# Attention's final scaling split in two, the first tile's inversion run beside the sample's heads, and token transposes ahead of score products

## What is computed

```python
h = rmsnorm(x); c = h @ w_in                       # RWKV columns | q, k, v | two gates
# A: RWKV-7 time mixing: a matrix state scanned over the tokens, per head
# B: differential attention, block-causal for the prompt
s = einsum(q, k) * d**-0.5; p = softmax(s)
o = einsum(p[:, 0] - lam * p[:, 1], v)             # per head
o = rmsnorm(o, subln) * (1 - lam_init)             # the "final scaling"
mix = sigmoid(gA) * (y_a @ w_out_a) + sigmoid(gB) * (o @ w_out_b)
x = x + rmsnorm(mix @ w_o)
x = x + rmsnorm((silu(u_g) * u_v) @ w_ffn_out)     # u_g, u_v = rmsnorm(x) @ w_ffn_in
```

## Time and profile before

| | |
|---|---|
| median of 3 runs | 1107.36 us (1107.15 to 1109.85) |
| the profiled execution's own time | 1107.29 us |
| its span, first to last instruction | 1105.5 us |
| TensorE busy | 1011.3 us (91%) |
| VectorE busy | 501.0 us (45%) |
| ScalarE busy | 276.5 us (25%) |
| GpSimd busy | 490.8 us (44%) |
| mean granted TensorE clock | 0.969 of 2.4 GHz |

### The profile page before, as it was taken

One profiled execution on the slowest core, in us unless ns is written; L12 is line 12 of the kernel. 1 busy time (PEld: TensorE's weight loads), 2 busy tenths in 40 slices (PEclk: granted clock), 3 DMA queues, 4 the chain that ended last, 5 costly groups with the idle time before them and its releaser, 6 DMA issues.

```text
span 1105.5 us, 21747 instructions
## 1 busy us (share of the span) xinstructions
PE 1011.3 (91%) x8886; PEld 954.9 (86%) x8886; DVE 501.0 (45%) x859; ACT 276.5 (25%) x768; POOL 490.8 (44%) x327
## 2 busy tenths in 40 slices
PE   4999998899958889989989994999999999999995
PEld 4999998887856777768789994999999999999994
DVE  5566798367565555554348317232332333200003
ACT  4223452255421222423221235110110111010111
POOL 3555564323233113142164550555655556556561
PEclk9999999999979999999999996999999999999997
DMA  8233323422212100002412531233232332332232
GB/s 240 72 90 83 77 77 97 120 59 70 78 60 60 35 2 31 31 13 75 156 49 71 183 95 39 58 94 88 83 95 77 94 89 81 88 89 85 74 86 82
DMA packets 137580, 89.15 MB, mean 81 GB/s; under 512 B 5242, under 2 KB 129504, under 8 KB 137504
## 3 DMA queue, kind: packets, MB, share of 16 engines
q1 hardware_dynamic: 128356, 70.42, 22.5%
q10 hardware_dynamic: 9148, 17.65, 4.5%
HBM read 78.86 MB, written 9.19 MB: 80 GB/s over the span
## 4 chain that ended last, share of the span: by engine, by line
PE 80%; DVE 12%; ACT 2%; issue 2%; POOL 1%; DMA 1%; DVEq 0%; ACTq 0%; POOLq 0%
PE dense L892 64%; PE side L944 4%; PE side L844 1%; PE side L818 1%; PE side L1064 1%; PE side L987 1%; PE side L874 1%; PE side L808 1%; PE side L1013 1%; DVE amax L1509 1%; DVE mb L1803 1%; PE side L839 1%; PE side L798 1%; DVE gain L1452 1%; DVE otok L1536 1%
## 5 line engine op out<-in xcount | busy, mean ns | idle before, releaser
L647 POOL TENSOR_SCALAR w_hi<-w_raw 128x1024 fp32r<-128x1024 f32 x127 | 139.2, 1096 | 484.5 <-PE dense L892 467.0
L650 POOL TENSOR_TENSOR w_lo<-w_raw,w_hi 128x1024 fp32r<-128x1024 f32 x127 | 311.7, 2455 | 10.6
L892 PE MATMUL dense<-h_hi,w_hi 128*128 128x272 f32 x1392 | 306.3, 298 | 10.1 <-DVE h_lo L1445 8.5
L892 PE MATMUL dense<-h_lo,w_hi 128*128 128x272 f32 x1392 | 296.1, 290 | 0.0
L892 PE MATMUL dense<-h_hi,w_lo 128*128 128x272 f32 x1392 | 294.9, 289 | 0.0
L892 PEld LDWEIGHTS dense<-h_hi,w_hi 128*128 128x128 f32 x1392 | 222.9, 191 | 20.1 <-DVE h_lo L1445 9.6
L892 PEld LDWEIGHTS dense<-h_lo,w_hi 128*128 128x128 f32 x1392 | 224.3, 191 | 0.0
L892 PEld LDWEIGHTS dense<-h_hi,w_lo 128*128 128x128 f32 x1392 | 223.4, 191 | 0.0
L892 PE MATMUL dense<-S,w_hi 128*128 128x272 f32 x960 | 162.0, 291 | 1.7 <-DVE S L1806 1.5
L892 PEld LDWEIGHTS dense<-S,w_hi 128*128 128x128 f32 x960 | 136.5, 189 | 2.5 <-DVE S L1806 2.0
L892 PE MATMUL dense<-S,w_lo 128*128 128x272 f32 x480 | 99.5, 289 | 0.0
(11 more groups left out here) (249 smaller groups left out, 1314.9 us busy)
## 6 DMA issues: line engine op xcount, KB each, us to landing
w_raw<-in_w_ffn_in SPq DMA_DIRECT2D x44, 512.0 KB, 3.8
w_raw<-in_w_in SPq DMA_DIRECT2D x43, 512.0 KB, 3.9
w_raw<-in_w_ffn_out SPq DMA_DIRECT2D x16, 448.0 KB, 3.6
gates<-gst ACTq DMA_DIRECT2D x16, 272.0 KB, 2.0
w_raw<-in_w_o SPq DMA_DIRECT2D x8, 512.0 KB, 3.8
w_raw<-in_w_ffn_out SPq DMA_DIRECT2D x8, 512.0 KB, 3.7
mb<-gates ACTq DMA_DIRECT2D x1, 2176.0 KB, 8.8
ga<-gates ACTq DMA_DIRECT2D x1, 2176.0 KB, 9.4
```

The source lines that it names most:

```text
L647: nc.gpsimd.tensor_scalar(w_hi[:, slot, :], w_raw[:, slot, :], 1.0, 0.0, ALU.mult, ALU.add).then_inc(hi_split, 1)
L650: nc.gpsimd.tensor_tensor(w_lo[:, slot, :], w_raw[:, slot, :], w_hi[:, slot, :].bitcast(F32), ALU.subtract).then_inc(w_split, 1)
L892: ins = pe.matmul(acc[:, hf, 0:HALF], w, r[:, hf * HALF:(hf + 1) * HALF], start=first and n == 0, stop=final and n == 2)
```

## The change

Three things in `schedule()`, with the handlers that belong to them. `oscale` becomes two steps: step 0 for the four prompt tiles (it waits for the last prompt head), step 1 for the sample. Tile 0's `sb0`, `xi` and the first 12 of its 15 inversion rows, together with `oA` of tiles 0 to 3, are woven into the rows of the sample's four heads; its last three rows (`wt` 3, `wm` 4, `wd` 4) stay behind the `ofin` steps. In each tile `tok` stands ahead of `sk`, and `xi` of the next tile behind both. The fillers go where the list below says: one behind each `ofin`, three instead of eight in tile 0's inversion, and in tiles 0 to 3 seven instead of five (one more ahead of `sb1`, one more in the weave). No instruction's shape changes.

```diff
     for i, th in enumerate(heads):
-        s += piece() + [("attP", *th)] + piece()
+        rows = [piece() + [("attP", *th)], piece()]
         if i + 1 < len(heads):
-            s += [("attC", *heads[i + 1])]
+            rows[-1] += [("attC", *heads[i + 1])]
         if i + 2 < len(heads):
-            s += [("attS", *heads[i + 2])]
-        s += piece() + [("attO", *th)]
-    s += [("oscale",)]
+            rows[-1] += [("attS", *heads[i + 2])]
+        rows += [piece() + [("attO", *th)]]
+        if th[0] < SAMPLE:
+            s += sum(rows, [])
+        else:
+            sample += rows
...
-    s += invert_head(0)
-    for n, st in enumerate(skew(NT, "oA", "ofin")):
-        s += [st] + filler(n % 2)
-    s += weave([[("init0",)]] + invert_rows(0), [filler(1) for _ in range(8)])
+    first = invert_rows(0)
+    scaled = [[("oA", t)] for t in range(SAMPLE)]
+    s += [("oscale", 0)] + invert_head(0) + weave(sample, first[:-3], scaled)
+    s += [("oscale", 1), ("oA", SAMPLE)]
     for t in range(NT):
-        s += (invert_head(t + 1) if t < SAMPLE else []) + both("sk", t) + both("tok", t) + filler(t == SAMPLE)
-        s += both("sb1", t) + both("gv", t) + both("wu", t) + filler(t == SAMPLE) + both("e", t) + filler(1)
+        s += [("ofin", t)] + filler(1)
+    s += weave([[("init0",)]] + first[-3:], [filler(1) for _ in range(3)])
+    for t in range(NT):
+        head = t < SAMPLE
+        s += (both("sb0", t + 1) if head else []) + both("tok", t) + both("sk", t) + (both("xi", t + 1) if head else [])
+        s += filler(1) + both("sb1", t) + both("gv", t) + both("wu", t) + filler(t == SAMPLE) + both("e", t) + filler(1)
         if t < SAMPLE:
-            s += weave(invert_rows(t + 1), state_rows(t), post_rows(t - 1) if t else [], [filler(1) for _ in range(4)])
+            s += weave(invert_rows(t + 1), state_rows(t), post_rows(t - 1) if t else [], [filler(1) for _ in range(5)])
...
             elif k == "oscale":
-                landed(act, ("attO", SAMPLE, BH - 1), "o")
-                A.mark(f_act(orms[:, 0:SAMPLE * BH], ossq[:, 0:SAMPLE * BH], ACT.Sqrt, scale=1.0 / BV, bias=EPS),
-                       s_["o_rms"], "o_rms")
-                A.mark(f_act(orms[0:DEC, SAMPLE * BH:], ossq[0:DEC, SAMPLE * BH:], ACT.Sqrt, scale=1.0 / BV, bias=EPS),
-                       s_["o_rms"], "o_rms")
+                n, a, b_ = ((P, 0, SAMPLE * BH), (DEC, SAMPLE * BH, NT * BH))[step[1]]
+                landed(act, ("attO", SAMPLE if step[1] else SAMPLE - 1, BH - 1), "o")
+                A.mark(f_act(orms[0:n, a:b_], ossq[0:n, a:b_], ACT.Sqrt, scale=1.0 / BV, bias=EPS), s_["o_rms"], "o_rms")
...
             elif k == "oscale":
-                dve.wait_ge(s_["o_rms"], 2)
-                V(vec.reciprocal(orst[:, 0:SAMPLE * BH], orms[:, 0:SAMPLE * BH]))
-                V(vec.reciprocal(orst[0:DEC, SAMPLE * BH:], orms[0:DEC, SAMPLE * BH:]))
+                n, a, b_ = ((P, 0, SAMPLE * BH), (DEC, SAMPLE * BH, NT * BH))[step[1]]
+                dve.wait_ge(s_["o_rms"], step[1] + 1)
+                V(vec.reciprocal(orst[0:n, a:b_], orms[0:n, a:b_]))
```

More of the change, by code:

```diff
@@ L237, in schedule @@
     s += [("attS", *heads[0]), ("attC", *heads[0]), ("attS", *heads[1])]
+    sample = []
     for i, th in enumerate(heads):
-        s += piece() + [("attP", *th)] + piece()
+        rows = [piece() + [("attP", *th)], piece()]
         if i + 1 < len(heads):
-            s += [("attC", *heads[i + 1])]
+            rows[-1] += [("attC", *heads[i + 1])]
         if i + 2 < len(heads):
-            s += [("attS", *heads[i + 2])]
-        s += piece() + [("attO", *th)]
-    s += [("oscale",)]
+            rows[-1] += [("attS", *heads[i + 2])]
[4 more added lines that the diff above has]
+            sample += rows
     fill = [dense("gA", i, p, 4) for i in range(8) for p in range(4)] + [dense("outB", i, p, 2) for i in range(8) for p in range(2)]
```

## The result

The changed kernel took 1103.09 us in the median of 10 runs (1096.13 to 1105.81), the kernel before 1109.92 us beside it (10 runs): a ratio of 0.994, 95% interval 0.9921 to 0.9959. It is faster, by 6.6 us instead of 19.7, and outside the range of 1078 to 1097 us. The profiled execution took 1105.81 us, span 1104.0 us, mean granted clock 0.956 (before 0.969). It is the slowest of the ten, so its profile shows more of what went wrong than the median does.

The account below looks back on a forecast made before the run. TensorE, busy 91% of the span, was taken as the bound, with its idle and low-clock time removable. Gains of 9.5 + 9.3 + 0.9 = 19.7 us off 1107.3 gave 1088 us, range 1078 to 1097.

Parts of the forecast that it names:

- `tok` ahead of `sk`, tiles 0 to 3: Prompt tiles' heads: four `gt` waits go, 7.3 us, with 0.9 + 1.1 us of low clock: 9.3 us gained.
- The failed step: Sample's stretch: a low clock follows the long wait at the first `wt`, costing 1.5 us.
- the forecast wait: Sample's stretch: TensorE waits 3.4 us at the first `wt` for `xp`.
- The idle time of the sample's stretch: TensorE's new idle time beside the sample's heads: 5.0 us behind VectorE and 3.4 us at `wt`, 8.4 us.
- the first part: Scaling and inversion moved beside the sample's heads: 19.4 us won less 9.9 us of new losses, net 9.5 us.
- the rival of the changed name: Tile heads: ScalarE's copies, or `xi` behind `gt`, are as late as `gt` was; 1097 us, chance 0.10.
- Each piece keeps its price: Fillers: a dense piece costs the same wherever it stands, so moving pieces was counted as no gain or loss.
- the margin that was called thin: Around `outB`: VectorE's 2.4 us wait for `mb` and its drains, 3.9 us, are covered by TensorE's 0.3 + 3.9 us.
- a sign of being wrong: In the changed profile, a wait ending at the load of `mb` (L1792) would show the forecast wrong.
- The end: End of the stage: `yfin` falls inside TensorE's last wait, 4.15 us for `y_lo`, gaining 0.9 us.
- the clock stays low through the mixed stretch: Rival: sample's heads to inversion's end, 15 pieces and 7 us of small work, all at low clock; 1113 us, chance 0.03.
- the sample's stretch gives all back: Rival: new losses in the sample's stretch equal the 19.4 us won there; 1097 us, chance 0.13.

Follow-up runs that it names:

- old head order: Changed kernel with only the tile heads' order undone (`xi`, `sk`, `tok` again) in all tiles: 0.9959 of the kernel before, 1102.41 us.
- 0.9898: Changed kernel with `sk` ahead of `tok` in tile 4 alone, tiles 0 to 3 keeping the new order: ratio 0.9898 to the kernel before, 1097.56 us.
- both measurements of the change: The changed kernel measured, then again without any edit: 0.994 (1103.09 us) and 0.9936 (1100.65 us) of the kernel before.
- twelve pieces: Kernel with `sk` first in tile 4 and four pieces per weave, plus a dense piece in each of the sample's twelve rows: 0.9817, 1089.71 us.
- four-piece weaves: Kernel with `sk` first in tile 4, weaves of tiles 0 to 3 cut from five pieces to four, the rest at the stage's end: 0.9908, 1097.31 us.
- three pieces ahead: Kernel with a piece in each of the sample's twelve rows, three pieces moved from the stage's end ahead of tile 4's score products: 0.9795, 1086.28 us.

## Why the prediction was wrong

The ratios add up to the result in three terms:

| term | forecast | measured | from |
|---|---|---|---|
| scaling and inversion, fillers, end of the stage | 9.5 + 0.9 | 4.6 | old head order, 0.9959 |
| `tok` ahead of `sk`, tiles 0 to 3 | 9.3 | 6.8 | 0.9898 against 0.9959 |
| `tok` ahead of `sk`, tile 4 | 0 | -4.4 | 0.9938 (mean of both measurements of the change) against 0.9898 |
| sum | 19.7 | 7.0 | |

Each is uncertain by 1.6 to 2.5 us, from the intervals.

- **The failed step is the clock.** "A wait of that length is followed by a low clock, as both long waits were: 1.5 us" ties the low clock to long waits, and so gives tile 4 none and the sample's stretch one short spell. The runs showed three things against it. First, no long wait is needed: in tile 4 the clock fell after a start with no wait over 0.97 us, and stayed up longer where a single wait of 1.48 us stood in front of dense work. Second, the forecast wait, that at the first `wt`, isn't the cause in the sample's stretch: filling it left the low clock at 13.7 us, and with twelve pieces it stands unfilled and there is no low clock at all, in three profiles. Third, the second of the two spells there followed a wait of 2.1 us in a place that the forecast didn't name. *The Trainium skill (TensorE: Matmul & The Clock Gate, A second HAM failure mode: psum-queue depth-cycling) describes a kernel, of another shape and type, whose frequent short idles between groups of matmuls make the clock swing; the trace agrees, with 2.24 us busy of 3.30 in front of 17 us at 0.51.*
- **Its price in the sample's stretch** comes from busy times. With twelve pieces and no low clock TensorE was busy 47.2 us; less five pieces of 1.63 that is 39.1 us for the changed kernel's work. It took 42.6, 43.6 and 45.0 us with 6.8, 10.2 and 13.7 us at the low clock: 3.5, 4.5 and 5.9 us, a little under half of the time at the low clock, against the forecast 1.5. The kernel before has the same matmuls in this stretch as the one with twelve pieces and was busy 50.6 us, so its low clock cost 3.3 us, about the 3.5 that the forecast had counted as won. The time at the low clock is about that of before (13.7); but the low clock of before lay partly in idle time, where it cost nothing, and the new one lies in full work. So instead of winning 2.0 us, the clock of this stretch lost 0.2 to 2.6.
- **The size of tile 4's term** was never in the sum. I read the head's order only where it had a `gt` wait, and tile 4 has none: its `tok` is short, ScalarE is late with a store there, and putting `tok` first draws `sk` behind ScalarE's copies: one wait of `tok` of 0.97 us, three of `sk` of 0.52, 0.26 and 0.26. Small waits, 2.0 us in all and no more idle time in the stretch than before, but strung together.
- **The idle time of the sample's stretch** was right in sum, 8.06 us against 8.4, and wrong in place. The first `wt` cost 2.2 us in two waits (1.36 and 0.86), not 3.4. The longest single wait was that of a product `wd` behind VectorE (2.1 us at 312.17), for this reason:

```profile
300.34 1.14 DVE L1542 SCALAR_TENSOR_TENSOR otok<-otok,orst,subln 128x128 f32<-128x128 f32 x4
...
307.48 4.09 DVE L1542 SCALAR_TENSOR_TENSOR otok<-otok,orst,subln 128x128 f32<-128x128 f32 x8
311.60 0.76 DVE L1664 TENSOR_TENSOR gain<-side,cst 128x256 f32<-128x256 f32 x2
```

  Eight scalings stood in VectorE's queue ahead of the drain that TensorE waited for. Four took 1.14 us, eight 4.09 instead of 2.3, since one split of GpSimd (2.38 us from 307.07) fell on them. The forecast had bounded that collision at one split of 2.5 us, and it was one. VectorE's sum was overestimated elsewhere: L1452's successor took 0.43 us a piece, not 0.70. The `ofin` stretch and the last three inversion rows, costed at nothing, lost 0.50 and 0.70 us, which the 8.06 contain.
- **The place of the scaling carries the first part** (1.000 with all scalings behind the sample's root; no run put them behind the rows but ahead of that root). The cover of four pieces in front of the sample's own scaling held: its transpose waits 0.5 us where 3.55 stood, and for a bank (`o_lo` L1451), not for the scaling.
- **The heads of tiles 0 to 3**: the `gt` waits went as forecast. `sk` doesn't wait for ScalarE there. A wait of up to 0.8 us for `rb` at `gv` took a part of the place, 1.4 us in sum, as `xi` now stands ahead of `sb1`'s drain on VectorE; the rival of the changed name had that mechanism with a fifth of its price. The 2.0 us of low clock that the forecast tied to the `gt` waits don't go with them: with the old head order all four stand (7.3 us) and tiles 0 to 3 have no low clock, and the changed kernel has 10.2 us of it there without them. These two are more than the 2.5 us missing, within the intervals.
- **Each piece keeps its price** held by the time for five against four pieces in the weaves, and failed for the place that mattered: five pieces cost 8.2 us at the end and 0.7 us in the sample's stretch.
- **The load of `mb`** used up the margin that was called thin. In the changed kernel VectorE waits 1.98 us for it (forecast 2.4) at 514.32, a wait that the forecast had named as a sign of being wrong, and TensorE 0.83 us behind VectorE's next drain, where nothing had been counted. With a shorter weave it collided with another transfer, in a place that I hadn't named, the store of tile 3's state (6 us).
- **The end** gained 0.5 us (wait for `y_lo` 3.63 instead of 4.15), not 0.9.

Of the rivals, *the clock stays low through the mixed stretch* came nearest to the mechanism, with a chance of 0.03. It didn't hold as priced, 15 pieces all low; about a quarter of the stretch was low, and another spell stood in tile 4. That the sample's stretch gives all back didn't come.

What stays open: what lowers the clock of tile 4 in the kernels with four-piece weaves. With `sk` first they had 10.2 us there, in and behind a wait of 7.67, and 17.1 us with twelve pieces in the sample and a wait of 3.17; with five-piece weaves and a wait of 1.48 it was 3.4. No run changed that wait alone; the kernel with three pieces ahead removed the wait and thickened the start together. In the sample's stretch the second spell goes with the 2.1 us wait, but one run alone took that wait away without adding pieces, and what brings on the first, no run separated from the thin products around it. Of the first term's missing 5.8 us the clock covers 2.2 to 4.6 and the end 0.4; the idle time covers none, as it fell by about what was forecast. That leaves 0.8 to 3.2 us, which the intervals allow, and the split itself is read from profiles of single executions.

## What to carry to other kernels

Removing waits can leave a stretch of short waits with little work for TensorE in it; read the granted clock of every stretch that a reordering thins, also in the tiles where the removed wait never stood, since a low clock there can nearly double the time of the work behind it. Independent dense pieces are worth most in such a stretch: the same five pieces cost an estimated 8.2 us at the end and 0.7 us there, where they filled 4.0 us of idle time and took away 3.5 us of low clock. And when pieces move, look at what their completion triggers: here a load of 2176 KB slid in front of a small store whose landing an engine waited for.

## What the runs showed of the hardware

- TensorE's granted clock fell after a thin start of tile 4 (2.24 us busy of 3.30, no wait over 0.97 us before it), and stayed at 1.2 GHz for 17.00 us in which TensorE was busy for 16.93 us. With one wait of 1.48 us and dense work behind it (6.90 us busy of 7.20) it was low for 3.6 us. A piece of 12 matmuls took 2.88 us there and 1.63 us at the full clock.
- Six more products in the thin start, of no use to the result, took tile 4's time at the low clock from 17.1 (13.7 in a second profile) to 3.4 us and its length from 40.63 (38.74) to 36.71 us.
- A 64 KB store issued 4.0 us behind a 2176 KB load on ScalarE's queue held ScalarE for 7.22 us in one kernel and 7.95 in another; with the load 21.8 and 33.0 us ahead ScalarE waited 1.77 and 3.45 us for it.
- Identical code ahead of the change took between 289.2 and 292.9 us by execution, with 3.4 to 17.1 us at the low clock, so a gain of some us can't be read from two profiles.
